# Seven products over six of sixteen contraction tiles in the MLP pairs of a decoder trunk

## What is computed

```python
def sqrelu_mlp(h, w_up, w_down):
    return jnp.square(jax.nn.relu(h @ w_up)) @ w_down

def reference(...):
    h = x
    for layer in range(DEPTH):
        ...
            h = h + fox_mixer(rmsnorm(h, fox_norm[j]), ...)
        ...
            h = h + retention_mixer(rmsnorm(h, ret_norm[j]), ...)
        h = h + sqrelu_mlp(rmsnorm(h, mlp_norm[layer]), mlp_up[layer], mlp_down[layer])
    return rmsnorm(h, final_norm)
```

## Time and profile before

| | us |
| --- | --- |
| three runs | 2490.51, 2487.20, 2487.61 |
| median | 2487.61 |
| span of the profiled execution | 2485.3 |
| TensorE busy | 2474.5 |
| VectorE busy | 1915.0 |
| ScalarE busy | 1402.3 |

### The profile page before, as it was taken

The page is one execution under the profiler, slowest core; times in us unless marked ns, Lnnn a source line. Parts: engine busy times, 40 slices in busy tenths (PEclk is TensorE's granted clock), DMA queues, the critical chain, the costliest instruction groups (busy, mean ns, idle before and its releaser), DMA issues.

```text
span 2485.3 us, 30031 instructions
## 1 busy us (share of the span) xinstructions
PE 2474.5 (100%) x11128; PEld 2050.7 (83%) x11128; DVE 1915.0 (77%) x2118; ACT 1402.3 (56%) x1689; POOL 158.6 (6%) x272
## 2 busy tenths in 40 slices
PE   9999999999999999999999999999999999999998
PEld 7888888888888888888888888888888888888887
DVE  6455555887978888987778868778988888788787
ACT  7454445554646555655556545656565555464564
POOL 0000000100100000101110001000010000010010
PEclk9999999999999999999999999999999999999999
DMA  8445456675756766766665665666677666666584
GB/s 312 158 155 182 140 200 218 214 253 182 260 202 222 248 208 229 237 212 204 219 225 184 231 201 183 199 206 233 236 248 245 207 231 229 211 237 237 192 273 146
DMA packets 148503, 534.83 MB, mean 215 GB/s; under 512 B 18704, under 2 KB 18960, under 8 KB 147472
## 3 DMA queue, kind: packets, MB, share of 16 engines
q1 hardware_dynamic: 131040, 476.65, 55.1%
q0 software_dynamic: 17184, 56.11, 7.9%
q10 hardware_dynamic: 144, 0.26, 0.0%
HBM read 506.74 MB, written 26.21 MB: 214 GB/s over the span
## 4 chain that ended last, share of the span: by engine, by line
PE 53%; DVE 2%; issue 1%; DMA 1%; ACT 1%; POOL 0%; DVEq 0%; ACTq 0%; POOLq 0%
PE acc L905 9%; PE acc L907 9%; PE acc L906 9%; PE sc L907 7%; PE sc L906 7%; PE sc L905 7%; PE mix L906 1%; PE mix L907 1%; PE mix L905 1%; DVE w_lo L1916 1%; ACT w_hi L1339 0%; DMA raw<-in_w_stream 0%; DMA evac<-park 0%; PE tr L1054 0%; PE tr L703 0%
## 5 line engine op out<-in xcount | busy, mean ns | idle before, releaser
L1916 DVE TENSOR_TENSOR w_lo<-raw,w_hi 128x1024 fp32r<-128x1024 f32 x696 | 847.1, 1230 | 290.4 <-ACT w_hi L1339 287.8
L1339 ACT ACTIVATE w_hi<-raw 128x1024 fp32r<-128x1024 f32 x696 | 727.8, 1058 | 571.8 <-PE sc L907 185.3
L905 PE MATMUL acc<-w_hi,xT_hi 128*128 128x512 f32 x826 | 322.6, 391 | 1.0 <-DVE xT_lo L1981 0.6
L907 PE MATMUL acc<-w_hi,xT_lo 128*128 128x512 f32 x826 | 321.6, 389 | 0.0
L906 PE MATMUL acc<-w_lo,xT_hi 128*128 128x512 f32 x826 | 321.5, 389 | 0.0
L1339 ACT ACTIVATE w_hi<-scratch 128x1024 fp32r<-128x1024 f32 x201 | 211.8, 1057 | 169.3 <-PE acc L907 74.4
L1916 DVE TENSOR_TENSOR w_lo<-scratch,w_hi 128x1024 fp32r<-128x1024 f32 x201 | 244.7, 1220 | 68.1 <-ACT w_hi L1339 67.5
L905 PE MATMUL sc<-w_hi,xT_hi 128*128 128x512 f32 x736 | 287.4, 390 | 0.0
L907 PE MATMUL sc<-w_hi,xT_lo 128*128 128x512 f32 x736 | 286.6, 389 | 0.0
L906 PE MATMUL sc<-w_lo,xT_hi 128*128 128x512 f32 x736 | 286.4, 389 | 0.0
L905 PE MATMUL acc<-w_hi,aT_hi 128*128 128x512 f32 x600 | 233.8, 390 | 0.0
(11 more groups left out here) (279 smaller groups left out, 3930.5 us busy)
## 6 DMA issues: line engine op xcount, KB each, us to landing
raw<-in_w_stream SPq DMA_DIRECT2D x725, 512.0 KB, 4.6
scratch<-in_w_stream SPq DMA_DIRECT2D x171, 512.0 KB, 4.8
park<-stage POOLq DMA_DIRECT2D x38, 512.0 KB, 3.2
evac<-park POOLq DMA_DIRECT2D x152, 128.0 KB, 3.2
gain<-in_gains POOLq DMA_DIRECT2D x4, 1024.0 KB, 8.1
qk_park<-evac POOLq DMA_DIRECT2D x8, 512.0 KB, 4.8
scratch<-qk_park POOLq DMA_DIRECT2D x32, 128.0 KB, 5.3
h<-in_x SPq DMA_DIRECT2D x2, 1024.0 KB, 8.7
```

The costliest lines, as they stand in the source:

```text
L905: pe.matmul(bank[:, :], x_hi, w_hi[:, c], start=start, stop=False, skip_group_check=True)
L907: return pe.matmul(bank[:, :], x_lo, w_hi[:, c], start=False, stop=stop, skip_group_check=True)
L1339: act.activation(w_hi[:, slot * SW:(slot + 1) * SW], mlp_raw(u, load_of(u, t)), ACT.Copy).then_inc(mlp_hi, 1)
L1916: dve.tensor_tensor(w_lo[:, c], mlp_raw(u, load_of(u, t)), w_hi[:, c].bitcast(F32), ALU.subtract).then_inc(mlp_lo, 1)
```

## The change

All MLP pairs but the very first (15 of the first MLP, 16 of the second) become `WIDE_PAIR`:

- Six contraction tiles instead of four go through seven products, each now 3 contraction tiles (9 matmuls, 1536 weight columns). Ten tiles stay plain, in weight tiles of three or two units of 512 columns: (3, 3, 2, 2) per block, in `LATE` pairs and in the first pair of the second MLP all of two. The order of the products is B11, TAU1, TAU2, B21, TAU3, B22, TAU4. TensorE's order has 93 matmuls fewer.
- The parts are summed in PSUM. Where before a product bank was copied out and added at the end, a bank is now seeded and the next products add to it: ScalarE copies x to `mix[0]` ahead of TAU2 (`seed_u`), `mix[1]` to SBUF (`copy_p5`) and `mix[0]` to z ahead of TAU3 (`seed_z`); VectorE writes e = p5 - mix[0] ahead of B22 (`seed_e`) and w = p5 - z ahead of TAU4 (`seed_w`). The three parts, the sums of them into `tr` and the folds into `h` are gone from the MLP pairs.
- The ring is 14 units of 512 columns (seven slots) in the MLPs, 12 in retention. A tile that crosses the ring's end is copied and subtracted in two pieces. Raw tiles have five places of 1536 columns, so a load has up to 768 KB.
- The third weight sum (`tau3`) is made just ahead of B21's low part, in place of right behind the first.
- S1 to S4 grow to three contraction tiles each and no longer fit two slots: they lie in pieces in the ring's first slots, in other buffers' free columns, and for down pairs partly in `aT`'s blocks of token 1. So in i mod 4 = 1 ScalarE's copies of them wait for the low part of the second turned quad (`turn_out`, turn + 2).
- Gains are loaded by quads into other buffers' free columns; the loops over blocks ahead of the first MLP are written out.

The core of the diff:

```diff
-RING = 6
-RING_AT = SLOTS - RING
...
+RING_AT = 2
...
+W_B11, W_TAU1, W_TAU2, W_B21, W_TAU3, W_B22, W_TAU4 = range(SEVEN)
...
+KT_SEVEN, KT_WIDE = 4, 6
+LEFT, RIGHT = (0, 1, 4), (2, 3, 5)
...
+RAW_WIDE = 5
...
+    if u in LATE:
+        return [Rest(half, kt, 2) for kts in ((6,), (8, 10), (12, 14)) for half in range(2) for kt in kts]
+    if u == mlp_unit(1, 0):
+        return [Rest(half, kt, 2) for half in range(2) for kt in range(KT_WIDE, KT, 2)]
+    return [Rest(half, kt, n) for half in range(2) for kt, n in ((6, 3), (9, 3), (12, 2), (14, 2))]
...
-            add(first if i == 0 else SEVEN_PAIR, sums + 1 if i % 4 < 2 else sums + 2 + i // 4)
+            add(first if i == 0 else WIDE_PAIR, sums + 1 if i % 4 < 2 else sums + 2 + i // 4)
...
-    mlp(SUPER + 4, SEVEN_PAIR)
+    mlp(SUPER + 4, WIDE_PAIR)
...
+RING_UNITS_MLP, RING_UNITS_RET = 14, 12
...
+                pe.wait_ge(x_out, unit.pairs)
+                block_sum(u, W_B11, x, lambda kk: x_part(lhs, 0, LEFT[kk]), True, True)
+                pe.wait_ge(s_lo, unit.sums)
+                wait(pe, v_made, unit.sevens)
+                wait(pe, p5_out, unit.wides)
+                wait(pe, o_out, TOKS * heads_done)
+                block_sum(u, W_TAU1, mix[1], lambda kk: s_part(u, S1, kk), True, True)
+                pe.wait_ge(u_seeded, unit.wides + 1)
+                block_sum(u, W_TAU2, mix[0], lambda kk: s_part(u, S2, kk), False, True)
+                block_sum(u, W_B21, x, lambda kk: x_part(lhs, 0, RIGHT[kk]), False, False)
+                pe.wait_ge(z_seeded, unit.wides + 1)
+                block_sum(u, W_TAU3, z, lambda kk: s_part(u, S3, kk), False, True)
+                pe.wait_ge(e_seeded, unit.wides + 1)
+                block_sum(u, W_B22, e, lambda kk: s_part(u, S4, kk), False, False)
+                pe.wait_ge(w_seeded, unit.wides + 1)
+                block_sum(u, W_TAU4, z, lambda kk: x_part(lhs, 1, RIGHT[kk]), False, False)
...
+            def seed_u(u, heads_done=0):
+                wait_used(act, u, W_B11)
+                wait(act, e_seeded, UNITS[u].wides)
+                wait(act, u_made, UNITS[u].sevens)
+                wait(act, o_out, TOKS * heads_done)
+                act.activation(mix[0][:, :], banks_of(u)[0][:, :], ACT.Copy).then_inc(u_seeded, 1)
+            def copy_p5(u):
+                wait_used(act, u, W_TAU1)
+                wait(act, w_seeded, UNITS[u].wides)
+                wait(act, squared, T("squared"))
+                act.activation(p5[:, :], mix[1][:, :], ACT.Copy).then_inc(p5_out, 1)
+                T.up("p5")
+            def seed_z(u):
+                wait_used(act, u, W_TAU2)
+                act.wait_ge(z_out, UNITS[u].pairs)
+                act.activation(banks_of(u)[1][:, :], mix[0][:, :], ACT.Copy).then_inc(z_seeded, 1)
...
+                hi(u, W_B11)
+                if by_pe:
+                    square_of_h(1, p_quad, z_out, done)
+                if was_up and not was_plain:
+                    relu(0, x_done, acc[0], x_out, done, turn)
+                    relu(1, z_done, acc[1], z_out, done, turn)
+                    relu_squared(0, x_out, done)
+                    relu_squared(1, z_out, done)
+                hi(u, W_TAU1)
+                hi(u, W_TAU2)
+                hi(u, W_B21)
+                if was_up:
+                    relu(0, e_done, sc[0], e_out, done, turn + 1)
+                    relu(1, w_done, sc[1], w_out, done, turn + 1)
+                    relu_squared(0, e_out, done)
+                seed_u(u, RET_HEADS * m)
+                hi(u, W_TAU3)
+                hi(u, W_B22)
...
+                copy_p5(u)
+                seed_z(u)
+                hi(u, W_TAU4)
+                hi(u, 7)
...
+                if new_sums:
+                    act.wait_ge(turn_out, turn + 2)
+                    s_high(new_sums)
...
+                dve.wait_ge(fetched, GRID * 16 * (n + 1))
+                step(dve.tensor_tensor(s[S1], a21, a22, ALU.subtract))
+                step(dve.tensor_tensor(s[S2], s[S1], a11, ALU.subtract))
+                dve.tensor_tensor(s[S3], a11, a21, ALU.subtract)
+                dve.tensor_tensor(s[S4], a12, s[S2], ALU.add).then_inc(s_made, 1)
...
+                dve.wait_ge(p5_out, unit.wides + 1)
+                dve.wait_ge(z_seeded, unit.wides + 1)
+                dve.wait_ge(e_out, unit.pairs)
+                dve.tensor_tensor(banks_of(u)[2][:, :], p5[:, :], mix[0][:, :], ALU.subtract).then_inc(e_seeded, 1)
+            def seed_w(u):
+                wait_used(dve, u, W_TAU3)
+                dve.wait_ge(w_out, UNITS[u].pairs)
+                z, w = banks_of(u)[1], banks_of(u)[3]
+                dve.tensor_tensor(w[:, :], p5[:, :], z[:, :], ALU.subtract).then_inc(w_seeded, 1)
...
+                lo(u, W_B11)
+                tau1(u)
+                if by_pe:
+                    gained_after(1, p_quad, z_out, done)
+                if turn is not None and not was_plain and not late_norm:
+                    turn_blocks(turn)
+                lo(u, W_TAU1)
+                tau2(u)
+                if was_late:
+                    add_bank(0, p_quad, acc[0], x_done, x_out, done)
+                    add_bank(1, p_quad, acc[1], z_done, z_out, done)
+                lo(u, W_TAU2)
+                if late_norm and not end:
+                    wait_gain(dve, 1)
+                    gained_after(0, p_quad, x_out, done)
+                    gained_after(1, p_quad, z_out, done)
+                tau3(u)
+                lo(u, W_B21)
+                tau4(u)
+                if late_norm and not end:
+                    turn_blocks(turn)
+                if not was_up:
+                    add_bank(0, p_quad + 1, sc[0], e_done, e_out, done, scaled=not by_pe)
+                lo(u, W_TAU3)
+                lo(u, W_B22)
+                seed_e(u)
+                if not was_up:
+                    add_bank(1, p_quad + 1, sc[1], w_done, w_out, done, scaled=not by_pe)
+                lo(u, W_TAU4)
+                if by_pe:
+                    dve.wait_ge(parked, 16 * (turn + 1))
+                if was_normed and not end:
+                    gained_after(0, p_quad + 1, e_out, done, stage if by_pe else tr)
+                seed_w(u)
+                if was_normed and not end:
+                    gained_after(1, p_quad + 1, w_out, done, stage if by_pe else tr)
+                if turn is not None and not by_pe:
+                    turn_blocks(turn + 1)
+                lo(u, 7)
+                lo(u, 8)
+                if turn is not None and not late_norm:
+                    if new_sums:
+                        wide_sums(turn, 0)
+                    turn_lo(turn, *dst, p_quad)
+                lo(u, 9)
...
+                for t in range(11, last):
+                    lo(u, t)
+                if turn is not None and late_norm:
+                    s_low(X_SUMS_OF_RET)
                 if turn is not None and not by_pe and not late_norm:
+                    if new_sums:
+                        wide_sums(turn + 1, 1)
                     turn_lo(turn + 1, *dst, p_quad + 1)
+                lo(u, last)
+                if new_sums:
+                    s_low(new_sums)
+                if turn is not None and late_norm:
                     turn_lo(turn + 1, *dst, p_quad + 1)
+                if not up and u not in LATE:
+                    add_bank(0, quad, acc[0], x_done, x_out, done + 1)
+                    if (m, i) != (0, PAIRS - 1):
+                        add_bank(1, quad, acc[1], z_done, z_out, done + 1)
```

More of the change, by code:

```diff
@@ L52 @@
 WF_COLS = KT * 2 * FOX_HEADS
[L53 removed]
 PAIRS = MLP_BLOCKS // 2
[L59 to L62 removed]
+RING_AT = 2
+UNITS_OF_SLOT = SW // NB
 SEVEN = 7
[L64 to L70 removed]
+B11, TAU1, TAU3, B21, TAU2, B22, TAU4 = range(SEVEN)
@@ new lines, in load_of, with is_sum @@
+def load_of(u, t):
+    unit = UNITS[u]
+    if t >= unit.products:
+        return t - unit.products + (4 if unit.products else 0)
+    if unit.kind == WIDE_PAIR:
+        return {W_B11: 0, W_TAU1: 0, W_TAU2: 0, W_B21: 3, W_TAU3: 1, W_B22: 2, W_TAU4: 0}[t]
+    return {B11: 0, TAU1: 0, TAU3: 1, B21: 3, TAU2: 0, B22: 2, TAU4: 0}[t]
+def is_sum(u, t):
+    kind = UNITS[u].kind
+    return (kind == WIDE_PAIR and t in (W_TAU1, W_TAU2, W_TAU3, W_TAU4)
+            or kind == SEVEN_PAIR and t in (TAU1, TAU2, TAU3, TAU4))
@@ L1334, in hi @@
                     act.wait_ge(w_used, T("block") * (SLOTS - 1) + (slot + 1))
-                if UNITS[u].kind == SEVEN_PAIR and t in (TAU1, TAU3, TAU2, TAU4):
+                if is_sum(u, t):
                     wait_sum(act, u, t)
```

911 lines of the change are left out of this document (513 added, 398 removed).

## The result

| | before | changed |
| --- | --- | --- |
| median, us | 2487.42 | 2591.59 |
| runs, us | 2487.2 to 2490.51 | 2586.89 to 2596.64 |
| span of the profiled execution | 2485.3 | 2585.1 |
| mean granted clock | 0.999 | 0.988 |

The ratio is 1.0418, with a 95% interval of 1.0403 to 1.0434: the change is 104 us slower. The forecast was 2496, from 2472 to 2510.

What follows compares the result with a forecast made beforehand. TensorE was taken as the bound, VectorE second at 83%. Stalls of 29.5 us against 21.1 removed gave + 8.4, a span of 2493.7, plus 2.3 to the median: 2496.0 us, range 2472 to 2510.

Steps and rivals of the forecast that it cites:

- Slower: Whole kernel: a time more than 0.2% (5 us) above the kernel before; chance 0.48.
- TensorE's part: MLP pairs: three matmuls fewer in each of 31 pairs at 0.2267 us, 21.1 us removed; new pair takes 41.48 us.
- VectorE's prices: VectorE: a 1536-column instruction takes 1.76 us and starts its successor after 1.67, bounds 1.60 and 1.74.
- rival 4: VectorE instructions don't overlap, 0.08 us more each: 36 us more, 2532 us; chance 0.01.
- i mod 4 = 0: Product phase, with i mod 4 = 3: VectorE's block ends late, 0.5 us stall at TAU4; 13 pairs together 6.5.
- i mod 4 = 2: Pairs inheriting lateness from i mod 4 = 1: waits 4.1 less slack 2.1, stall 2.0 us; 8 pairs, 16.
- term for the fetch: Second turned quad: 7.3 us from first quad's low part to ScalarE's copy; VectorE waits 0.5 to 1.1.
- the walk: Product phase timed from B11's start on TensorE: chain of copies, low parts and weight sums; TAU2's `lo` starts at -1.70.
- the seed of u: ScalarE's new copies in the product phase: hidden, 0.60 us each, the first starting at 2.24 and due at 3.9.
- Rival 3: 768 KB weight loads come late, from tile 8 in i mod 4 = 1: 8 to 16 us more, 2504 to 2512; chance 0.11.
- Pair 15: Last pair of the first MLP: gained copies and a transpose in VectorE's block, stall of 4.9 us.
- The third sum: Third weight sum, inside VectorE's solid block after TAU2's `lo`; that block stalls 0.5 us, 6.5 over 13 pairs.

Runs made afterwards that it cites:

- e1: Changed kernel, but in i mod 4 = 1 the second turned quad is read from buffer `stage` instead of after its way through DRAM; 2551.5 us, ratio 1.0238 to 1.0272.

## Why the prediction was wrong

- **Sign right, size not.** "Slower" had the largest chance (0.48), but the time lies 82 us above the top of the range.
- **TensorE's part** held: 93 matmuls fewer, 21.1 us, and 41.57 us in undisturbed pairs (41.48 said).
- **VectorE's prices** held. A 1536-column instruction takes 1.75 or 1.76 and its successor starts 1.67 later (845.22 - 843.55), as said (0.60 and 1.14 give 1.68 when added up). So rival 4 is out at this width too: the next operation starts 0.08 ahead of the end of the last. The rule of the Trainium skill (VectorE: DVE Perf Modes, The DRAIN you can't avoid) doesn't hold for these instructions; the same section says that an operation that isn't held starts earlier.
- **i mod 4 = 0** held: 3.8 us in six pairs for 3.
- **i mod 4 = 2 is the step that failed**, at its term for the fetch: "I take 7.3 in all, since that copy also stood in a queue". It took 12.0. 1.15 to the issue (0.9 said), because the park landed only then; 10.87 from there to the copy, where the earlier trace rows had 7.67 and I cut it to 6.4. VectorE was ready when the walk said (25.5 us into the pair, 25.2 said), so the wait was 5.2 and not 0.5 to 1.1. With that number alone the forecast's own sum for the pair gives 2.0 + 4.4 = 6.4 of stall, against waits of 4.4 to 6.2 and losses of 6.8 to 10.3 measured. The term is not all of the error: with this wait taken away (e1) the eight pairs still lost 39.1 us, where 16 was forecast.
- **What I took for hidden was not**: the seed of u, "due at 3.9", stands behind work that is late when the chain is. My walk had one queue (VectorE) run late and kept ScalarE's times as they were. The last quad of the pair was no term at all; TensorE waited 7.4 us for it, and 14.3 in e1.
- **Rival 3** had the right resource, DMA, and the wrong victim. It let the loads come late; the loads came (in pair 9 ScalarE's first wait for one, 1.3 us, is behind tile 8, and VectorE had no gap there), and made park and fetch late. Its own text put transfers of 768 KB "beside the fetches", and priced the loads only.
- **The clock** was no term. A stall was costed at its length; here stalls cost some 25 us more in all, 18.3 of them in i mod 4 = 2.
- **Pair 15**: 18.3 for 4.9. The ring restarts for retention on the place of the pair's last tile, which frees only with the whole pair; moving the start gave 7.9 back, the other 5.6 above the forecast are open. The whole diff showed the restart, and I called the place of B11 "as before" for all pairs.
- **The third sum** was walked only for a pair in time, 6.5 us for 13 pairs. Moving it gave 24.3 and 22.6 us, of which 3.3 lie in i mod 4 = 0, where the walk held; in late pairs the walk had it wrong by far more than its own term, and by which wait is open.
- Bounds: each came from the nearest row, but the fetch's upper bound (1.1 us of wait) was tighter than a row I had (7.67 instead of 6.4 gives 1.9), so the range could not reach.
